# The first loads of a decoder trunk: a new order of transfers and of the first transposes

## The reference

```python
def rms_norm(x, g):
    xf = x.astype(jnp.float32)
    y = xf * lax.rsqrt(jnp.mean(xf * xf, axis=-1, keepdims=True) + NORM_EPS)
    return (y * g.astype(jnp.float32)).astype(x.dtype)

def swiglu_ffn(h, w_up, w_down):
    gate, up = jnp.split(h @ w_up, 2, axis=-1)
    return (jax.nn.silu(gate) * up) @ w_down

x = x + 0.5 * swiglu_ffn(rms_norm(x, norm_ffn1[l]), ffn1_up[l], ffn1_down[l])
```

## Time and profile before

| What | us |
|---|---|
| median of 3 runs | 1089.81 (1089.68 to 1089.98) |
| the profiled execution's own time | 1089.43 |
| its span | 1087.6 |
| PE busy | 1079.0 |
| DVE busy | 888.4 |
| ACT busy | 652.9 |
| first real product on PE starts | 6.87 |

### The profile page before, as it was taken

How to read it: one execution, slowest core, us unless ns; L and a number is a source line. 1 busy time by engine, 2 the same in 40 slices (tenths; PEclk the granted TensorE clock), 3 DMA queues, 4 the chain that set the end, 5 groups by cost and what they waited for, 6 DMA issues and landing times.

```text
span 1087.6 us, 15435 instructions
## 1 busy us (share of the span) xinstructions
PE 1079.0 (99%) x5309; PEld 906.2 (83%) x5309; DVE 888.4 (82%) x1163; ACT 652.9 (60%) x832; POOL 78.9 (7%) x100
## 2 busy tenths in 40 slices
PE   9999999999999999999999999999999999999997
PEld 6888888988988888888888888888899888888886
DVE  6989988766987698988889988986678777988896
ACT  6656654656953565665565755646469446565664
POOL 0044410100200000000000000001012000000000
PEclk9999999999999999999999999999999999999999
DMA  8576584754455555655646567638444554656651
GB/s 291 178 237 217 170 313 161 253 164 128 161 184 164 174 193 193 203 183 193 218 145 217 177 207 262 238 125 278 139 143 156 193 175 155 220 167 196 222 169 69
DMA packets 140235, 207.44 MB, mean 191 GB/s; under 512 B 5224, under 2 KB 103728, under 8 KB 139680
## 3 DMA queue, kind: packets, MB, share of 16 engines
q1 hardware_dynamic: 137472, 196.89, 55.2%
q0 software_dynamic: 2144, 9.12, 2.2%
q10 hardware_dynamic: 576, 0.85, 0.2%
HBM read 205.66 MB, written 1.05 MB: 190 GB/s over the span
## 4 chain that ended last, share of the span: by engine, by line
PE 99%; DMA 1%; DVE 0%; issue 0%; ACT 0%; SPq 0%
PE psum L1681 31%; PE psum L1683 31%; PE psum L1682 31%; PE psum L1771 2%; PE psum L1699 1%; PE psum L1959 1%; PE psum L1763 1%; DMA raw<-ffn_up_dram 1%; PE psum L1973 0%; PE psum L2006 0%; PE psum L2008 0%; DVE xs L1253 0%; DVE x L1069 0%; SPq L508 0%; ACT scores L1053 0%
## 5 line engine op out<-in xcount | busy, mean ns | idle before, releaser
L1075 DVE TENSOR_TENSOR w_lo<-raw,w_hi 128x1024 fp32r<-128x1024 f32 (+6 forms) x279 | 412.1, 1502 | 76.1 <-ACT w_hi L684 75.4
L1681 PE MATMUL psum<-w_hi,xT 128*128 128x512 f32 (+2 forms) x984 | 383.0, 389 | 0.0
L1683 PE MATMUL psum<-w_hi,xT 128*128 128x512 f32 (+2 forms) x984 | 379.4, 386 | 0.0
L1682 PE MATMUL psum<-w_lo,xT 128*128 128x512 f32 (+2 forms) x984 | 379.0, 385 | 0.0
L684 ACT ACTIVATE w_hi<-raw 128x2048 fp32r<-128x2048 f32 (+5 forms) x167 | 284.5, 1710 | 72.0 <-PE psum L1683 67.2
L1681 PEld LDWEIGHTS psum<-w_hi,xT 128*128 128x128 f32 x984 | 184.8, 188 | 39.2 <-DVE w_lo L1075 0.9
L1683 PEld LDWEIGHTS psum<-w_hi,xT 128*128 128x128 f32 x984 | 184.7, 188 | 37.1
L1682 PEld LDWEIGHTS psum<-w_lo,xT 128*128 128x128 f32 x984 | 184.9, 188 | 34.4 <-issue 0.2
L801 ACT ACTIVATE oT<-xs 128x1024 fp32r<-128x1024 f32 x72 | 76.5, 1062 | 69.8 <-DVE xs L1075 69.8
L769 ACT ACTIVATE scores<-psum,stat 128x256 f32<-128x256 f32 x88 | 41.3, 473 | 111.0 <-PE psum L1683 110.1
L1075 DVE TENSOR_TENSOR oT<-xs,oT 128x1024 fp32r<-128x1024 f32 x72 | 87.9, 1227 | 0.0
(11 more groups left out here) (217 smaller groups left out, 1413.6 us busy)
## 6 DMA issues: line engine op xcount, KB each, us to landing
raw<-ffn_up_dram SPq DMA_DIRECT2D x170, 512.0 KB, 4.9
raw<-ffn_down_dram SPq DMA_DIRECT2D x44, 1024.0 KB, 4.9
raw<-w_in_dram SPq DMA_DIRECT2D x20, 1024.0 KB, 5.1
raw<-w_attn_proj_dram SPq DMA_DIRECT2D x8, 1024.0 KB, 5.0
raw<-w_out_dram SPq DMA_DIRECT2D x8, 1024.0 KB, 5.1
raw<-w_uq_dram SPq DMA_DIRECT2D x8, 576.0 KB, 4.2
gates<-b_gate_dram POOLq DMA_DIRECT2D x4, 1024.0 KB, 7.5
raw<-w_ukv_dram SPq DMA_DIRECT2D x8, 512.0 KB, 3.8
```

What stands on the lines that cost most here:

```text
L1075: return dve.tensor_tensor(dst, a, b, ALU.subtract)
L1681: nc.tensor.matmul(dst, a_hi, b_hi, start=first, stop=False)
L1682: nc.tensor.matmul(dst, a_hi, b_lo, start=False, stop=False)
L1683: return nc.tensor.matmul(dst, a_lo, b_hi, start=False, stop=last)
```

## The change

The identity becomes ScalarE's first load and the first rows its second; the second rows go to SyncE's queue, between quarters 1 and 2 of group 0; the norm row goes to GpSimd's queue, ahead of everything that GpSimd does. PE runs four warm-up matmuls instead of five, and turns the first rows before the norm row. The first of their four tiles goes to a bank of its own (bank 3); DVE multiplies it alone, then the other three, and PE's first product waits for that tile only. `turn_first(0, 1)` moves ahead of the wait for quarter 2.

```diff
-WARM, KEEP = 5, 3
+WARM, KEEP = 4, 3
+ALONE_BANK = 3
...
                 for k in range(4):
                     sp.dma_start(dst[:, k], src[:, k, :, 0:CH]).then_inc(first_landed[a][k], 16)
+                    if (a, k) == (0, 1):
+                        sp.dma_start(x[:, 1, half(0)], x_in[0, blk(1), half(0)]).then_inc(x_landed[0][1], 16)
...
-            sp.dma_start(first_gain, gains[0:1, :].rearrange("o (k n) -> (o k) n", k=KD)).then_inc(gain_row_landed, 16)
...
+            pool.dma_start(first_gain, gains[0:1, :].rearrange("o (k n) -> (o k) n", k=KD)).then_inc(gain_row_landed, 16)
             pool.memset(half_neg[:, :], -0.5).then_inc(exponent_set, 1)
...
-            for t in range(TB):
-                act.dma_start(x[:, t, half(0)], x_in[0, blk(t), half(0)]).then_inc(x_landed[0][t], 16)
-                if t == 0:
-                    act.dma_start(ident[:, :], c_ident).then_inc(ident_landed, 16)
+            act.dma_start(ident[:, :], c_ident).then_inc(ident_landed, 16)
+            act.dma_start(x[:, 0, half(0)], x_in[0, blk(0), half(0)]).then_inc(x_landed[0][0], 16)
...
+            def first_gained_alone():
+
+                dve.wait_ge(first_turned, 1)
+                dve.tensor_tensor(first_x(0, 0)[:, 0, :], psum[:, ALONE_BANK, 0:P],
+                                  gain_T[:, 0:1].to_broadcast([P, P]), ALU.mult).then_inc(first_ready, 1)
+                dve.wait_ge(norm_tr.sem, norm_tr.upto(0, quarter(0, 0, 0)))
+                dve.tensor_tensor(first_x(0, 0)[:, 1:, :], tr_view(NORM_T_BANK[0][0])[:, 1:, :],
+                                  gain_T[:, 1:4].unsqueeze(2).to_broadcast([P, 3, P]),
+                                  ALU.mult).then_inc(normed_sem(0, 0), 1)
...
-                first_gained(0, 0)
+                first_gained_alone()
...
             def turn_first(h, t):
                 pe.wait_ge(x_landed[h][t], 16)
-                tiles(psum[:, NORM_T_BANK[h][t], :], x[:, t, half(h)], 4, norm_tr)
+                if (h, t) == (0, 0):
+                    tiles(psum[:, ALONE_BANK, :], x[:, 0, 0:P], 1).then_inc(first_turned, 1)
+                    tiles(psum[:, NORM_T_BANK[0][0], P:], x[:, 0, P:4 * P], 3, norm_tr)
+                else:
+                    tiles(psum[:, NORM_T_BANK[h][t], :], x[:, t, half(h)], 4, norm_tr)
...
-                    wait(normed, 0, t + 1 - TB)
+                    if t == 0:
+                        pe.wait_ge(first_ready, 1)
+                    else:
+                        wait(normed, 0, t + 1 - TB)
                     for k in range(4):
+                        if k == 2:
+                            turn_first(t, 1)
                         if t == 0:
                             pe.wait_ge(first_landed[0][k], 16)
-                        if k == 2:
-                            turn_first(t, 1)
+                        if t == 0 and k == 1:
+                            wait(normed, 0, 1 - TB)
...
             keep_clock(4, WARM)
             pe.wait_ge(ident_landed, 16)
+            turn_first(0, 0)
             pe.wait_ge(gain_row_landed, 16)
             nc.tensor.transpose(psum[:, 1, 0:KD], first_gain, ident[0:KD, 0:KD]).then_inc(gain_turned, 1)
-            turn_first(0, 0)
             keep_clock(5, KEEP)
```

More of the change, by code:

```diff
@@ L245, in trunk @@
         first_hi, first_lo = sem("first_hi"), sem("first_lo")
+        first_turned, first_ready = sem("first_turned"), sem("first_ready")
         final_x, final_sq, final_part = sem("final_x"), sem("final_sq"), sem("final_part")
```

## The result

The changed kernel takes 1092.04 us (median of 18 runs, 1091.36 to 1093.06), the kernel before on the same chips 1089.89 (18 runs, 1089.43 to 1091.53). The ratio is 1.0019, with a 95% interval of 1.0012 to 1.0026: 2.15 us slower. The profiled execution has a span of 1089.8 us against 1087.6, so 2.2 of it are in the trace.

What follows compares the result with a forecast made beforehand. The prediction took PE's own instruction stream as the bound, its start set by weight quarter 0. A first product 0.5 us earlier, kept to about 0.3 by weight group 2, took 1089.81 to 1089.5 us; range 1088.9 to 1090.9.

Steps and rivals of the forecast that it cites:

- The sign: Whole kernel: faster, 1089.5 us against a median of 1089.81 before.
- Step (b): ScalarE's queue, identity first and rows of block 0 second: rows, sharing transfers evenly with quarter 0, land at 4.5 us.
- Rival A: Rows of block 0 land late, at 5.95 us; first product at 7.74, 0.9 late: 1090.7 us; chance 0.2.
- Step (c): PE and DVE before the first product: first tile alone, norm row turned after rows, one warm-up fewer; product possible at 6.3.
- The removed warm-up: PE's start: saves nothing by itself, since PE waits for the rows; no cover between 3.6 and 4.64 us.
- B: PE's clock stays at 1.2 GHz through keepers and first product: 1.52 less 0.5, 1.0 us late, 1090.8 us; chance 0.13.
- Step (a): Norm row to GpSimd's queue: quarter 0 issued at 0.73, landing 6.24, product possible at 6.38; norm row takes near 2.2 us.
- Rival D: Norm row on GpSimd's queue lands at 9.5 us; first product at 10.6, 3.7 late: 1093.5 us; chance 0.03.
- the path from the rows becomes no shorter: Rows to weighted tile: separate tile saves up to 0.40 us, norm row behind four transposes puts 0.70 ahead.
- Step (d): Second rows among SyncE's quarters: land near 7.6 us, needed at 8.1, so hidden; later SyncE issues go out 0.2 later.
- Step (e): Sum: first product 0.5 us earlier; weight group 2, slack 0.05, lands 0.3 earlier; about 0.3 kept: 1089.5 us.
- Rival C: First product starts earlier, but weight group 2 lands as before and PE loses the gain at 20.6: 1089.8 us; chance 0.17.

Runs made afterwards that it cites:

- Experiment 3: The changed kernel with ScalarE's two loads exchanged, rows of block 0 first and identity second: 1091.35 us, ratio 1.0014.
- Experiment 5: The changed kernel with the norm row first on SyncE's queue again, so that quarter 0 goes out at 1.22 us: 1090.93 us, ratio 1.0011.
- Experiment 1: The changed kernel with nine warm-up matmuls instead of four, transfers and order unchanged: 1090.13 us, ratio to before 1.0001.
- Experiments 7 to 9: The kernel before with the changed PE and VectorE order and four warm-ups, 1091.44 us; with four warm-ups only, 1089.89; with that order and five warm-ups, 1089.98.
- experiment 4: The kernel before with the changed kernel's queues alone; five warm-ups, norm row turned first, four tiles weighted together: 1092.01 us, ratio 1.0018.
- experiment 9: The kernel before with rows turned before the norm row and first tile weighted alone, five warm-ups, transfers as before: 1089.98 us, ratio 0.9999.
- experiments 10 and 11: The kernel before with second rows on SyncE and weight group 2 split in halves: 1089.89 us; the same with first tile alone and one keeper: 1089.84 us.
- experiment 6: The kernel before with only the second rows moved to SyncE, between quarters 1 and 2: 1090.03 us, ratio 1.0001.
- experiment 12: The changed kernel with rows first and identity second on ScalarE, and eight warm-ups: 1089.85 us, ratio 1.0002.
- experiment 8: The kernel before with four warm-ups instead of five, nothing else: median 1089.89 us, ratio 1.0002, in two groups.

## Why the prediction was wrong

*The bound* was read rightly: PE's chain sets the end, and the two traces differ by what happens ahead of the second rows' turn. *The sign* was wrong, and 1092.04 lies above the range.

*Step (b) failed first.* It let the rows share the transfers evenly with quarter 0, by bytes, and took 4.5; they landed at 5.50. Rival A's 5.95 was nearer, and had 0.2; by A's own sum a landing at 5.50 gives a first product at 7.29, 0.42 late. Experiment 3 shows that bytes are the wrong measure: 256 KB issued together with quarter 0 took 2.7 us, 64 KB issued 0.42 after it took 4.0. Experiment 5 fills in the middle: 3.5 us when the issues are 0.07 apart. What is issued behind the first weight quarter lands late, whatever its size, and within about 0.3 us of that quarter itself: rows and norm row at 5.50 and 5.65 beside 5.3 in the changed kernel, identity and norm row at 5.11 and 5.25 beside 4.9 in experiment 3. One rival is not excluded: GpSimd issued a load at 1.25 in the changed kernel and in experiment 3, and none in experiment 5. Against it as the whole cause, the second rows of the kernel before went out 0.42 behind quarter 0 without it and took 4.8 us. Which part of the machine holds them back was not tried; that stays open.

*Step (c) failed with it, and is the larger part.* "The removed warm-up saves nothing by itself ... its cover is gone" saw the place, but rivals A and B were priced as two cases that exclude each other, each at about 1.0 us. They are one: late rows make PE's idle time 2.0 us instead of 1.0, and the clock then stays low until near 10 us. The sum is: turns 1.03 for 0.70, which with the late landing puts the tile's readiness at 7.56 (7.46 and 0.1) instead of the 6.87 of quarter 0, 0.69 late (0.33 of it by the slow turns); keepers until 8.51, 0.95 more; four records in 2.44 for 1.96, 0.48 more. That is 2.12, beside 2.13 in the chain and 2.15 in the medians. The chain puts the product's start at the keepers' modelled end; by the records it is at 8.30, which moves 0.2 us from the keepers to the product and leaves the sum. Experiment 1 shows the clock's share by giving 1.9 of it back without touching a transfer. B's price for the clock, 1.52 before the 0.5 of an earlier start was taken off, was about right in size (0.95 and 0.48 are 1.43).

*The removed warm-up* was priced in step (c) only through the idle time behind it. Experiments 7 to 9 show that it also costs by itself, with every load on time: 1.7 us, in four executions of eleven, and 1.8 in six of eleven. With the rows late it changes nothing: experiment 4, with the fifth warm-up, takes 1092.01.

*Step (a).* Quarter 0 went out at 0.73 and landed near 5.3, better than the 6.24 taken; it did not help. The norm row landed at 5.65, after 4.4 us, not 2.2; GpSimd issued it at 1.25. In the changed kernel it is needed at 6.65 and stays hidden; with the old order of turns it is the one that PE waits for (experiment 4). Rival D's size did not occur.

*Step (c), the tile.* 0.29 us, as taken. That the path from the rows becomes no shorter was misread: its own terms give 1.55 us from PE's start to the weighted tile (0.70, 0.49, 0.07, 0.29), and the earlier trace rows have 1.95 (4.01 to 5.96). In experiment 9 it is 1.76, 3.88 to 5.64. It was worth nothing there (1089.98, and 1090.03 for before) because quarter 0 sets the start.

*Step (d)* held: second rows and quarters were in time in the changed kernel. Where the start is really early they are not (experiments 10 and 11).

*Step (e).* The slack of 0.05 us on group 2 fits experiment 6, where a split 0.29 later made PE wait. The gain of 0.3 has no ground: it is the difference between an issue 0.49 earlier, of quarters 0 and 1, and one 0.2 later, of everything behind them, and group 2 is behind them. In the changed kernel its second load goes out at 8.53 and takes 7.7 us, before at 8.42 and 7.7: near 16.2 and 16.1, no gain. Experiment 1, with the same transfers, splits it from 16.45, experiment 12 from 15.92, so a shift of 0.3 can't be told from one execution to the next. In the changed kernel the split comes at 17.84 without a wait for the transfer: group 2 held nothing up. Rival C, at 0.17, has the time that this change shows without the clock (1090.13), but not by its mechanism: in experiment 1 the start was late, and PE did not wait for group 2. The rule of the Trainium skill that rival C names ("DMA: Bandwidth & Descriptors", section "Issuing engines are not separate DMA queues") fits the time of experiment 6, where 256 KB moved from one queue to another for nothing; it does not give the late landings of step (b).

## What to carry to other kernels

When a start-up path hands PE its first work later, price the idle time and the clock as one case: here rows that landed 2.1 us later than before (5.50 for 3.43) cost 2.1 us with the clock, and 0.1 to 0.3 without it (experiment 1). Issue what PE needs first ahead of the first bulk transfer of any queue, or in the same moment as first of its own queue, but not behind it, and don't judge its landing by bytes. And before spending work on an earlier start, look for the next transfer without slack; in this kernel early starts of 0.6 to 1.4 us in three versions (experiments 6, 10 and 11) were all lost within 15 us. Look at all the times, too, and not only at the median: experiment 8 has the median of the kernel before and four late executions in eleven.

## What was not expected of the hardware

- A 64 KB transfer on ScalarE's queue took 2.4 us when the first 256 KB weight quarter followed it and 3.96 when the quarter preceded it by 0.42 us; a 256 KB one took 2.7, 3.5 and 4.4 us for an issue together with it, 0.07 ahead of it as the second of its queue, and 0.42 behind it. In the cases of 3.96 and 4.4 us GpSimd had issued a load too.
- The clock's rise is not the same in every execution. With four warm-up matmuls and all loads on time the eleven times fall in groups of seven and four, or of five and six, with medians 1.7 and 1.8 us apart (1089.78 and 1091.45; 1089.91 and 1091.76); with a fifth one all eleven lie within 1.1 us (experiment 9), and three of 116 of the kernel before are as late. That the clock's rise parts them was seen in one execution of each kernel, and not in all.
- Taking filling away moved the rise back: without keepers PE idled 0.59 us more before the first product, and its records shorten only after 12 us, with the keepers near 10. That is one execution of each kernel; with the keepers and the rows first (experiment 3) it was near 11.6.
